# Neighbourhood attention by pairs of heads beside later projections

## The reference

```python
qkv = (h @ w_qkv).reshape(bsz, rows, GRID_W, 3, NA_HEADS, NA_HEAD_DIM)   # 16 heads of 64
q = rmsnorm(qkv[:, :, :, 0], q_norm) * (NA_HEAD_DIM ** -0.5)
k = rmsnorm(qkv[:, :, :, 1], k_norm)
v = qkv[:, :, :, 2]
...
s = jnp.einsum('bxqhd,brxkhd->bhxqrk', q_blk, k_blk).astype(jnp.float32)
s = s + bias                     # by head, row and column; -inf outside the window
pr = jax.nn.softmax(...)
o = jnp.einsum('bhxqrk,brxkhd->bxqhd', pr, v_blk)
...
return out @ w_out
```

## Time and profile before

| | us |
|---|---|
| median of 3 runs | 1698.72 (1698.44 to 1699.04) |
| the profiled execution | 1698.75 |
| its span in the trace | 1696.8 |
| PE busy | 1681.7 (99%) |
| DVE busy | 1076.4 (63%) |
| ACT busy | 899.8 (53%) |
| POOL busy | 73.6 (4%) |
| attention stage, from the first tile of w_qkv to the next feed-forward part | about 882 to 1020 |

### The profile page before, as it was taken

How to read it: one execution, slowest core, us unless ns; L and a number is a source line. 1 busy time by engine, 2 the same in 40 slices (tenths; PEclk the granted TensorE clock), 3 DMA queues, 4 the chain that set the end, 5 groups by cost and what they waited for, 6 DMA issues and landing times.

```text
span 1696.8 us, 22995 instructions
## 1 busy us (share of the span) xinstructions
PE 1681.7 (99%) x9366; PEld 1436.2 (85%) x9366; DVE 1076.4 (63%) x1332; ACT 899.8 (53%) x1279; POOL 73.6 (4%) x79
## 2 busy tenths in 40 slices
PE   8999999999999999999999999999999999999998
PEld 7888899998788888888888678888889999988886
DVE  5554688889975545755456866555655578776643
ACT  6443567777864435644355656444553456655432
POOL 0000000000100000000002500000000000000000
PEclk9999999999999999999999999999999999999999
DMA  9555566666466655776555226554565533555551
GB/s 307 187 181 179 168 189 191 194 199 192 152 202 195 197 167 180 194 237 207 179 168 199 87 75 202 183 192 163 192 196 160 165 105 121 173 191 183 184 185 64
DMA packets 243977, 300.58 MB, mean 177 GB/s; under 512 B 9248, under 2 KB 175520, under 8 KB 243872
## 3 DMA queue, kind: packets, MB, share of 16 engines
q1 hardware_dynamic: 238224, 289.25, 53.6%
q10 hardware_dynamic: 5648, 9.85, 2.0%
HBM read 297.96 MB, written 1.11 MB: 176 GB/s over the span
## 4 chain that ended last, share of the span: by engine, by line
PE 85%; DVE 10%; ACT 3%; issue 1%; DMA 0%; ACTq 0%; DVEq 0%
PE bank L561 81%; PE bank L564 4%; DVE wlo L1843 4%; DVE bc L1846 3%; DVE xTs L1846 1%; DVE EW L1843 1%; ACT whi L1326 1%; ACT EW L1323 1%; DMA h<-in_x 0%; ACT hThi L1326 0%; ACT bc L1323 0%; ACT L1583 0%; DVE Er L1843 0%; ACT gate L1323 0%; DMA cum<-ct 0%
## 5 line engine op out<-in xcount | busy, mean ns | idle before, releaser
L1843 DVE TENSOR_TENSOR wlo<-raw,whi 128x2048 fp32r<-128x2048 f32 (+2 forms) x284 | 620.6, 2190 | 344.2 <-ACT whi L1326 344.2
L1326 ACT ACTIVATE whi<-raw 128x2048 fp32r<-128x2048 f32 (+2 forms) x284 | 518.2, 1832 | 249.9 <-PE bank L561 246.2
L561 PE MATMUL bank<-whi,hThi 128*128 128x512 f32 x1072 | 425.5, 397 | 0.0
L561 PE MATMUL bank<-wlo,hThi 128*128 128x512 f32 x1072 | 418.3, 390 | 0.4 <-DVE wlo L1843 0.4
L561 PE MATMUL bank<-whi,hTlo 128*128 128x512 f32 x1072 | 403.0, 390 | 0.0
L561 PE MATMUL bank<-hThi,whi 128*128 128x256 f32 x888 | 253.3, 285 | 0.0
L561 PE MATMUL bank<-hThi,wlo 128*128 128x256 f32 x888 | 251.2, 283 | 0.0
L561 PE MATMUL bank<-hTlo,whi 128*128 128x256 f32 x888 | 251.2, 283 | 0.0
L561 PEld LDWEIGHTS bank<-whi,hThi 128*128 128x128 f32 x1072 | 201.6, 188 | 43.0 <-issue 3.2
L561 PEld LDWEIGHTS bank<-whi,hTlo 128*128 128x128 f32 x1072 | 201.5, 188 | 43.1 <-DVE hTlo L1846 0.3
L561 PEld LDWEIGHTS bank<-wlo,hThi 128*128 128x128 f32 x1072 | 201.7, 188 | 41.6 <-DVE wlo L1843 1.9
(11 more groups left out here) (214 smaller groups left out, 1883.2 us busy)
## 6 DMA issues: line engine op xcount, KB each, us to landing
raw<-in_ffn_w_gu SPq DMA_DIRECT2D x172, 512.0 KB, 4.8
raw<-in_ffn_w_down SPq DMA_DIRECT2D x40, 1024.0 KB, 5.0
raw<-in_w_in SPq DMA_DIRECT2D x30, 1024.0 KB, 5.2
raw<-in_ssd_w_in SPq DMA_DIRECT2D x16, 1024.0 KB, 5.6
raw<-in_ssd_w_in SPq DMA_DIRECT2D x32, 512.0 KB, 5.4
raw<-in_w_up SPq DMA_DIRECT2D x16, 1024.0 KB, 5.3
raw<-in_w_down SPq DMA_DIRECT2D x16, 1024.0 KB, 4.9
raw<-in_na_w_qkv SPq DMA_DIRECT2D x12, 1024.0 KB, 5.1
```

The lines of the kernel that those rows point to most:

```text
L561: return T.e.matmul(out, lhsT, rhs, start=start, stop=stop, skip_group_check=skip)
L1326: return e.activation(out, in_, ACT.Identity, **kw)
L1843: return e.tensor_tensor(out, a, b, op)
```

## The change

- The order of chunks becomes q, k, v of heads 0 to 7 (chunks 0, 2, 4), then q, k, v of heads 8 to 15 (1, 3, 5). The tiles of w_out are ordered (0,0), (1,0), (0,1), (1,1) in (columns, rows).
- Chunks 0, 2, 4 are done as before, but the transposes of the chunk before stand between the two tiles of a chunk and no longer behind it.
- The rest is a new `na_steps` of 18 steps. In each, PE has half a tile (`half`, 12 matmuls of 512 columns, all of one token half) of the remaining projections, with attention work for pairs of heads around it. The last four quarter pieces of w_out stand behind it (`out_part`).
- Scores, transposes and values go by pairs. The two heads' score matmuls alternate (rows 0 to 63 and 64 to 127 of the array, two banks), and so do their value matmuls (columns 0 to 63 and 64 to 127, one bank).
- The banks of the attention are 4 to 7 only (8 before); 0 to 3 hold the projections.
- POOL's bias gets 8 buffers (3 before); the outputs of heads 0 to 7 go to new tiles, since `hThi` and `hTlo` are still in use. The statistics get 4 slots.
- DVE computes sums of squares and means for both token halves before it multiplies either. The bias' addition and the maximum stay two instructions for a head, as before.
- The transposes of the residual, `turn(6, 0, 0)` and `turn(6, 1, 0)`, follow the last piece of w_out. On DVE the preparation of the tile ahead (`take`, 9) stands ahead of all residual additions.

The numbers and kinds of instructions stay the same but for the order. The core of the diff:

```diff
+    for n in range(18):
+        if n in (0, 2, 4, 6):
+            if n >= 4:
+                yield "values", n // 2 - 2
+            yield "scores", n // 2
+        elif n in (3, 5, 7, 9):
+            yield "turn", (n - 3) // 2
...
+    yield "values", 7
+    yield "split", 7
+    yield "take", 9

 def na_banks():
-    rot, out = Rot(4, 5, 6, 7, 0, 1, 2, 3), {}
+    rot, out = Rot(4, 5, 6, 7), {}
...
+            def scores(p):
...
+                for t in range(2):
+                    for j in range(2):
+                        z = slice(64 * j, 64 * j + 64)
+                        done = mm(bank_half(nabank["scores", p, j], t), qT[z, p, t * P:(t + 1) * P], kT[z, p, :], True, True)
...
+            def values(p):
...
+                for kt in range(2):
+                    for j in range(2):
+                        hd = 2 * p + j
+                        done = mm(banks[b][64 * j:64 * j + 64, 0:256], v[:, kt, hd * 64:hd * 64 + 64], pt[:, j, kt * 256:kt * 256 + 256],
+                                  kt == 0, kt == 1, True)
+                done.then_inc(*sig("values", p))
+                empties[b] = ("oTlo", p)
...
+            out_part(0, (2,))
+            out_part(1, (2,))
+            out_part(0, (3,))
             residual_in(6, 0, (0, 1))
+            out_part(1, (3,))
+            residual_in(6, 1, (2, 3))
             turn(6, 0, 0)
             turn(6, 1, 0)
-            closing_block([("nout", 1, 1)], (2, 3), hThi, hTlo, 4)
-            residual_in(6, 1, (2, 3))
             ple_first(1, 0)
```

More of the change, by code:

```diff
@@ L16 @@
 BIG = 1e30
+TOP = 3e38
 NRAW, NSPL = 4, 3
@@ L250, in na_steps, with tile_half @@
 def na_steps():
[L253 to L258, removed]
+    def tile_half(n):
+        t = n % 2
+        return ("qkv", (1, 1, 3, 3, 5, 5)[n // 2], n // 2 % 2, t) if n < 12 else ("nout", (n - 12) // 2, 0, t)
+    for n in range(18):
[5 more added lines that the diff above has]
+            yield "turn", (n - 3) // 2
+        elif n in (8, 10):
+            yield "values", n // 2 - 2
+        if n in (7, 10):
+            yield "transposes", (0, 1)[n == 10]
+        if n == 11:
+            yield "scores", 4
+        elif n == 12:
+            yield "scores", 5
+        elif n == 13:
+            yield "turn", 4
+            yield "scores", 6
+        elif n == 14:
+            yield "values", 4
+            yield "turn", 5
+        elif n == 15:
+            yield "values", 5
+            yield "scores", 7
+        elif n == 16:
+            yield "turn", 6
+        elif n == 17:
+            yield "values", 6
+            yield "turn", 7
+        if n < 16:
+            yield "half", tile_half(n)
+        else:
+            yield "first", n - 16
+        if n in (4, 8):
+            yield "means", (0, 1)[n == 8]
+        if n in (0, 2, 4, 6):
+            yield "logits", n // 2
+        if n in (11, 12, 13, 15):
+            yield "logits", n - 7 - (n == 15)
+        if n in (0, 2, 4, 6, 8, 10, 12, 14, 16):
+            yield "take", n // 2
+        if n in (0, 2, 4, 6):
+            yield "exps", n // 2
+        if n in (11, 12, 13, 15):
+            yield "exps", n - 7 - (n == 15)
+        if n in (4, 8):
+            yield "unit", (0, 1)[n == 8]
+        if n in (1, 3, 5, 7):
+            yield "normalise", n // 2
+        if n in (12, 13, 14, 16):
+            yield "normalise", n - 8 - (n == 16)
+        if n in (3, 5, 7, 9):
+            yield "evict", (n - 3) // 2
+        if n in (13, 14, 16, 17):
+            yield "evict", (4, 5, 0, 6, 7)[n - 13]
+        if n in (4, 6, 8, 10):
+            yield "split", n // 2 - 2
+        if n in (14, 15, 17):
+            yield "split", (4, 5, 0, 6)[n - 14]
+        if n in (7, 10):
+            yield "gains", (0, 1)[n == 10]
+        if n == 12:
@@ new lines, in na_banks @@
+    for what, x in na_steps():
+        if what in ("scores", "turn"):
+            for j in range(2):
+                out[what, x, j] = rot.take()
+        elif what == "transposes":
+            for j in range(2):
+                out[what, x, j] = rot.take()
+        elif what == "values":
+            out[what, x] = rot.take()
+        elif what == "logits":
+            for j in range(2):
+                rot.give(out["scores", x, j])
+        elif what == "evict":
+            for j in range(2):
+                rot.give(out["turn", x, j])
+        elif what == "gains":
+            for j in range(2):
+                rot.give(out["transposes", x, j])
+        elif what == "split":
+            rot.give(out["values", x])
@@ L1106, in natt @@
-            for what, hd in na_steps():
-                if what == "scores":
[L1108 to L1113, removed]
+                    empties[pair(i)[t]] = ("v", 0, t) if c6 == 4 else ("qn", c6 // 2, 0, t)
+            def scores(p):
+                for j in range(2):
+                    clear(nabank["scores", p, j])
+                for which in range(2):
+                    T.wait_ge(*at("qkTs", which, p // 4, p % 4 // 2))
+                for t in range(2):
+                    for j in range(2):
+                        z = slice(64 * j, 64 * j + 64)
+                        done = mm(bank_half(nabank["scores", p, j], t), qT[z, p, t * P:(t + 1) * P], kT[z, p, :], True, True)
+                        if t:
+                            done.then_inc(*sig("nscore", 2 * p + j))
+                for j in range(2):
+                    empties[nabank["scores", p, j]] = ("nbias", 2 * p + j)
@@ new lines, in out_part @@
+            def out_part(c, ks):
+                label = ("nout", c, 1)
+                if 0 in ks:
+                    held[label] = take(*label)
+                for k in ks:
+                    for t in range(2):
+                        last = products(label, k, t, False, k == 3)
+                        if k == 3:
+                            last.then_inc(*sig(*half(label, t)))
+            for what, x in na_steps():
+                if what == "scores":
+                    scores(x)
@@ L1114, in natt @@
                 elif what == "turn":
-                    turn_p(hd)
+                    turn_p(x)
                 elif what == "values":
-                    values(hd)
-            xw = [(("oThi", k), ("oTlo", k)) for k in range(8)]
-            token_block(("nout", 0, 0), ("nout", 0, 1), (0, 1), hThi, hTlo, xw)
+                    values(x)
+                elif what == "transposes":
+                    transposes(x, 1, [nabank["transposes", x, j] for j in range(2)])
+                elif what == "half":
+                    half_tile(*x)
+                elif what == "first":
+                    out_part(x, (0, 1))
@@ L1638, in values @@
                     copy(mem["nv"][:, t, chunk(c)], banks[bs[t]], scale=rstd(5, t)).then_inc(*sig("v", c, t))
-            for c6 in range(5):
-                which, c = c6 // 2, c6 % 2
-                b2 = (2 * c6 % 4, 2 * c6 % 4 + 1)
+            for i, c6 in enumerate(NA_CHUNKS[:3]):
                 for k in range(2):
                     take("qkv", c6, k)
[L1645 to L1666, removed]
+                if i:
+                    with_gains(i - 1, 0, (4 + 2 * (i - 1), 5 + 2 * (i - 1)))
@@ new lines, in natt @@
+                if c6 == 4:
+                    values(0, pair(i))
+                else:
+                    squares(i)
+            tiles = [("qkv", c, k) for c in NA_CHUNKS[3:] for k in range(2)] + [("nout", c, k) for c, k in NA_OUT]
+            for what, x in na_steps():
+                if what == "take":
+                    take(*tiles[x])
+                elif what == "means":
+                    squares(3 + x)
+                elif what == "gains":
+                    with_gains(x, 1, [nabank["transposes", x, j] for j in range(2)])
@@ L1667, in natt @@
                 elif what == "keep":
-                    values(1, (2, 3))
+                    values(1, pair(5))
                 elif what == "exps":
[L1670 to L1678, removed]
@@ L2184, in natt, with unit @@
                     e.tensor_scalar(mv, sv, 1.0 / 64, EPS, ALU.mult, ALU.add).then_inc(*sig("qms", which, c, t))
+            def unit(i):
+                c6 = NA_CHUNKS[i]
+                which, c = c6 // 2, c6 % 2
+                for t in range(2):
+                    slot = 2 * which + t
+                    rv = st[:, 104 + 8 * slot:112 + 8 * slot]
                     V.wait_ge(*at("qrs", which, c, t))
-                    if c6 >= 2:
-                        V.wait_ge(*at("qkT", (c6 - 2) // 2, c6 % 2, 1))
```

296 lines of the change are left out of this document (173 added, 123 removed).

## The result

The changed kernel takes 1706.14 us (1704.15 to 1707.35, 6 runs) beside 1698.88 for the kernel before (6 runs): ratio 1.0043, 95% interval 1.0033 to 1.0053. It is slower by 7.3 us. The forecast was 1704.0, with a range of 1694 to 1710.

What follows compares the result with a forecast made beforehand. TensorE, busy for 1681.7 of 1696.8 us, was taken as the bound. 1698.75 less 16.7 for the pairs plus 18.25 of waits gave 1700.3, and 4.0 for the clock made 1704.3 (range 1694 to 1710).

Steps and rivals of the forecast that it cites:

- What the pairs give: Attention on TensorE: doing heads by pairs, with fewer cuts of the dense stretch, saves 16.7 us without any wait.
- step 5, bank 6: Turn 1's second head waits 3.6 us for bank 6, which split 0 frees behind logits, weight tile and multiplications.
- step 7, bank 7: Turn 2's second head waits 2.25 us for bank 7, which split 1 frees behind logits and weight tile.
- step 13, pair 4 normalised: Turn 4 waits for the normalised weights of heads 8 and 9, behind logits and weight tile: 2.95 us.
- step 14, pair 4 evicted: Values 4 wait 1.95 us for both evictions, which ScalarE has behind exponentials 6.
- the end, tile ahead of the residual: After the third out_part, take 9 stands ahead of the residual additions on VectorE; the residual's transposes wait 4.8 us.
- The clock: Lower granted clock behind the three waits of about 3 us and more (steps 5, 13, the end): 4.0 us.
- The clock holds: Rival: the waits don't lower the clock, giving 1700.3 us, within 0.2% of before; chance 0.22.
- A backlog that the first wait pays off: Rival, steps 4 to 16: VectorE's lateness is one backlog, later waits half as long, 1694.3 us; chance 0.16.
- Worse: Rival: every wait over 1 us lowers the clock and POOL's bias slows VectorE's tiles, 1710 to 1713; chance 0.10.
- Heads don't overlap: Rival: alternating heads don't overlap, 8 x 2.1 us come back, some inside the waits, 1715 us; chance 0.04.
- bank 4 is 0.1 late: Step 15: TensorE finds bank 4 freed 0.1 us late.

Runs made afterwards that it cites:

- e7: Changed kernel with the reorderings of e1, e2, e3, plus q's first transposes behind chunk 2, POOL's powers ahead of later bias, step 14 reordered: 1683.26 us, ratio 0.9906.
- e4: Changed kernel with each pair's score and value matmuls ordered head by head, no longer alternating: 1706.67 us, ratio 1.0045.
- e5: Changed kernel with useless dense matmuls filling four of TensorE's waits: 1701.88 us, ratio 1.0017; repeated, 1701.43 us beside 1705.34 for the unaltered changed kernel.
- e2: Changed kernel with splits 0, 1 and 5 right behind their step's logits, ahead of the weight tile: 1696.10 us, ratio 0.9983.
- e1: Changed kernel with the last tile's preparation (take 9) moved behind the first residual additions: 1699.51 us, ratio 1.0003.
- e3: Changed kernel with pairs 4 and 5 normalised ahead of the next pair's logits, pair 4 evicted ahead of pair 6's exponentials: 1702.21 us, ratio 1.0019.
- e8: Kernel before with only the scores and the values of two heads following each other, nothing else moved: 1698.18 us, ratio 0.9996.

## Why the prediction was right

- **What the pairs give.** Forecast 16.7 us on TensorE without waits. e7 has 1.3 us of waits and no slow stretch and is 16.6 us shorter in the stage: 17.9. In this, as in the forecast, the 1.5 us of waits and the slow stretch of the kernel before are part of what goes. The prices were 1.12 for scores (measured 1.06), 1.05 for values (1.01), 0.93 for a turn (0.79 between dense stretches). The row of eight records in 1.14 us was enough for the scores: what happened once in the kernel before happens with every pair here, in either order (e4).
- **The waits.** Each was foreseen with its place and its cause:

| place | forecast | measured |
|---|---|---|
| transposes of q, inside chunk 2 | 1.45 | 1.20 |
| transposes of k, inside chunk 4 | 0 (0 to 0.5) | 0.50 |
| step 5, bank 6 | 3.6 | 3.28 |
| step 7, bank 7 | 2.25 | 1.95 |
| step 13, pair 4 normalised | 2.95 | 2.89 |
| step 14, pair 4 evicted (and 0.1 at step 15) | 2.05 | 1.13 |
| step 16, bank 7 | 1.15 | 1.28 |
| the end, tile ahead of the residual | 4.8 | 4.23 |
| sum | 18.25 | 16.5 |

The sum of prices held to about 0.3 us in five of the eight places. At steps 5 and 7 what is too much is the 0.3 that I charged for POOL's bias beside the weight tile: the tiles of steps 4 and 6 take 2.28 us beside it, no longer than without. The end was put 0.6 too high. Step 14 is furthest off, and it shows the chain: behind step 13 TensorE was slow, so its half tile hid more of ScalarE's work; with the clock up, in e5 and e4, the same wait is 2.06 and 2.05. At chunk 4 POOL's bias stood ahead of the second powers, which I had at the edge.

- **The clock.** This term was rightly placed but built wrongly. I charged three drops of 1.5 us less something hidden, 4.0; there were four in both profiles (step 7's wait of 1.95 us had one as well). Compared with the same stretches in e5 they cost 1.4, 1.6, 2.4 and 1.5 us, 6.8 in all, of which 0.9 came back in the shorter wait of step 14. The medians say 4.3 and 3.9; the profiled executions are those with the lowest granted clock of their sets. The forecast's 4.0 agrees with the medians partly by luck. And the row that I took for a wait without cost, the 1.93 us in layer 0, has a slow stretch behind it in nine profiles of twelve, so it said less than I read from it.
- **The sum.** 128.5 - 17.9 + 16.5 + 6.8 is 133.9, and the stage takes 135.5. Most of the last 1.6 us is how a wait is counted: from the end of the instruction before it, which lies 0.1 to 0.2 behind the time at which the next could have started, eight times. The profiled execution took 1706.53 us where 1704.3 was forecast, and that it came so near is partly luck: the gain was put 1.2 too low and the waits 1.8 too high, while the clock was put 2.8 too low, and these 1.6 and the 0.9 of layer 0 weren't in the sum.
- **The rivals.** "The clock holds" (1700.3) is what e5 shows: 1701.4 to 1701.9. "A backlog that the first wait pays off" is refuted by e2 and e1: none of the later waits was halved, and taking early waits away changed only that at values 4, by 0.7, with the clock. "Worse" fails on both counts: seven waits exceed 1 us and four lowered the clock, and beside POOL's bias some early tiles are slower (2.77 us at 901.63) but not those of steps 4 and 6, for which TensorE waits. "Heads don't overlap" is refuted by the first rows. That a filled or removed wait uncovers the next one happened once (e3, 3 us): 2.0 of them at scores 7, in a place that my walk had found to be just in time ("bank 4 is 0.1 late"), and 1.1 at values 5, which it hadn't named.

The Trainium skill, "TensorEngine Tiling (Array Packing)", section Tiling Modes, has tiles that run in parallel and a drain at a change of mode. The first is seen in every pair; what a change costs beyond the 0.1 us on either side of a dense stretch, no run here shows. The Trainium skill, "TensorE: Matmul & The Clock Gate", section "Why this matters for your kernels", advises to keep TensorE from idling between dense stretches. The case agrees that idling can cost the clock (e5), but with shorter gaps than that section warns of: here a wait of 1.95 us was followed by 1.2 GHz in both profiles of the changed kernel. And such a gap isn't always harmful: e8 has nine waits of up to 2.0 us without it, and e3 one of 3.28.

## What to carry to other kernels

When work is interleaved to hide it, write down for every step what stands ahead of it on each other engine: a 0.4 us step that frees a bank cost 3.3 us behind a 2.2 us weight tile, and moving it by one line gave it back. Put what frees a buffer, and what TensorE asks for next, ahead of what prepares work for later; preparation whose slot isn't free yet is the worst thing to have in front. A saving on the engine that is full counts only where the second engine has room (e8), so do the overlap and the interleaving together and then look at the waits one by one, since each can also cost clock behind it.

## What the hardware showed unexpectedly

- Two heads' float32 matmuls in different halves of the array overlap fully whether they alternate or follow each other: 1.06 and 1.07 us for a pair's scores in the two orders, 1.05 for one head.
- TensorE kept busy with useless matmuls through its waits makes the whole launch 4 us shorter than left idle (1706.1 to 1701.9, and 1705.3 to 1701.4), with the same dependencies.
- The same wait behind the same instructions can lower the clock in one execution and not in the next: in layer 0 some 1.9 us, with a slow stretch behind it in nine profiles of twelve.
- With waits of about 1.5 to 2.0 us in every 5 us and TensorE busy for 3.3 of 5, the granted clock stayed at 1.00 through the stage (e8), while single waits of 1.95 us between dense stretches were followed by 1.2 GHz in both profiles of the changed kernel. What tells them apart wasn't tried, and with one profile of e8 chance isn't ruled out.
